# Turned tiles handed on by halves, modulated tiles by inner tile, and the expert routing pulled ahead of the rounds' loop

## The reference

```python
# first block, two layers
for layer in range(2):
    y = mixer_block(x, ...)                         # projections, four branches, gates, output projection
    x = layer_norm(ALPHA * x + y, ln_g[layer, 0], ln_b[layer, 0])
    y = swiglu(x, ffn_w1, ffn_w3, ffn_w2) if layer == 0 else moe_ffn(x, ...)
    x = layer_norm(ALPHA * x + y, ln_g[layer, 1], ln_b[layer, 1])

def moe_ffn(x, router_w, router_b, w1, w3, w2):      # 8 experts, 2 for each token
    logits = x @ router_w + router_b
    top_val, top_idx = top_k(logits, 2)
    weights = softmax(top_val)
    return sum over experts of combine[e] * swiglu(x, w1[e], w3[e], w2[e])

# second block, two layers
for l in range(2):
    sh_a, sc_a, g_a, sh_f, sc_f, g_f = split(silu(c) @ w_mod[l] + b_mod[l], 6)
    h = rms_norm(x, norm_mix[l]) * (1 + sc_a) + sh_a
    x = x + g_a * (attention(h @ w_in[l]) @ w_out[l])
    h = rms_norm(x, norm_ffn[l]) * (1 + sc_f) + sh_f
    x = x + g_f * ((silu(h @ w_gate[l]) * (h @ w_up[l])) @ w_down[l])
```

## Time and profile before

| What | Value |
|---|---|
| Time of three runs, median (lowest to highest) | 2186.43 us (2185.7 to 2187.35) |
| The profiled execution's own time | 2190.64 us |
| Its span | 2188.7 us |
| Mean granted TensorE clock, share of full speed | 0.983 |
| Busy: PE, DVE, ACT, POOL | 96%, 40%, 17%, 4% |
| DMA | 421.44 MB, mean 193 GB/s |

### The profile page before, as it was taken

The page is one execution under the profiler, slowest core; times in us unless marked ns, Lnnn a source line. Parts: engine busy times, 40 slices in busy tenths (PEclk is TensorE's granted clock), DMA queues, the critical chain, the costliest instruction groups (busy, mean ns, idle before and its releaser), DMA issues.

```text
span 2188.7 us, 37442 instructions
## 1 busy us (share of the span) xinstructions
PE 2093.4 (96%) x16270; PEld 1554.7 (71%) x16270; DVE 874.8 (40%) x1695; ACT 374.0 (17%) x891; POOL 78.2 (4%) x180
## 2 busy tenths in 40 slices
PE   9998999999999989999999999899999999999998
PEld 8787786877688867866543554387687768858786
DVE  1415435677724164342010000235466753444443
ACT  1312230000113132301010000133300012431000
POOL 3000000000000000020000000000000020000000
PEclk9999899999999998998999999999999999999999
DMA  8334234588563342337999999852468764233452
GB/s 259 111 99 149 80 123 166 194 302 288 179 194 97 97 164 77 106 99 254 347 319 363 342 336 346 298 170 97 173 234 290 264 197 134 97 116 111 159 173 96
DMA packets 333831, 421.44 MB, mean 193 GB/s; under 512 B 27222, under 2 KB 282148, under 8 KB 333668
## 3 DMA queue, kind: packets, MB, share of 16 engines
q1 hardware_dynamic: 312464, 352.96, 49.7%
q0 software_dynamic: 13408, 50.66, 6.6%
q10 hardware_dynamic: 7796, 15.43, 2.0%
HBM read 417.90 MB, written 1.05 MB: 191 GB/s over the span
## 4 chain that ended last, share of the span: by engine, by line
PE 85%; DVE 5%; DMA 5%; ACT 3%; issue 1%; ACTq 1%; SPq 0%; DVEq 0%; POOL 0%; POOLq 0%
PE psum L1276 14%; PE psum L1308 13%; PE psum L1415 11%; PE psum L1283 9%; PE psum L1293 9%; PE psum L1475 5%; PE psum L1939 3%; DMA ring<-in_w_up 3%; PE psum L1546 3%; PE psum L1721 2%; PE psum L1320 2%; DMA ring<-in_ffn_w 2%; PE psum L1749 1%; PE psum L1404 1%; PE psum L1488 1%
## 5 line engine op out<-in xcount | busy, mean ns | idle before, releaser
L1276 PE MATMUL psum<-xT,ring 128*128 128x256 f32 x1600 | 368.0, 390 | 6.4 <-ACT small L778 4.1
L1276 PEld LDWEIGHTS psum<-xT,ring 128*128 128x128 f32 x1600 | 307.9, 195 | 60.3 <-issue 6.6
L1293 PE MATMUL psum<-ring,arena 128*128 128x512 f32 x528 | 232.1, 593 | 0.0
L1283 PE MATMUL psum<-ring,xT 128*128 128x256 f32 (+2 forms) x960 | 202.5, 369 | 8.7 <-DVE xT L2668 3.9
L1283 PEld LDWEIGHTS psum<-ring,xT 128*128 128x128 f32 x960 | 172.4, 192 | 35.4 <-DVE xT L2668 4.2
L1293 PEld LDWEIGHTS psum<-ring,arena 128*128 128x128 f32 x528 | 97.9, 190 | 111.8 <-issue 111.6
L2115 DVE SCALAR_TENSOR_TENSOR arena<-arena,cond 128x512 f32<-128x512 f32 x168 | 126.3, 752 | 5.5
L1415 PE MATMUL psum<-ring,arena 128*32 128x256 f32 x2304 | 126.8, 379 | 0.7 <-DVE arena L2250 0.7
L1308 PEld LDWEIGHTS psum<-xT,ring 128*128 128x128 f32 x960 | 111.2, 192 | 19.0 <-issue 19.0
L1308 PE MATMUL psum<-oT,arena 128*128 128x128 f32 x960 | 117.6, 276 | 7.0 <-DVE arena L2130 7.0
L1308 PEld LDWEIGHTS psum<-oT,arena 128*128 128x128 f32 x960 | 112.0, 192 | 8.0 <-DVE arena L2130 8.0
(11 more groups left out here) (417 smaller groups left out, 2528.1 us busy)
## 6 DMA issues: line engine op xcount, KB each, us to landing
ring<-in_w_in SPq DMA_DIRECT2D x80, 1024.0 KB, 5.7
ring<-in_exp_w SPq DMA_DIRECT2D x312, 256.0 KB, 6.2
arena<-in_w_mod POOLq DMA_DIRECT2D x48, 1024.0 KB, 9.3
ring<-in_ffn_w SPq DMA_DIRECT2D x33, 1024.0 KB, 7.1
arena<-in_exp_w SPq DMA_DIRECT2D x120, 256.0 KB, 7.0
ring<-in_w_gate SPq DMA_DIRECT2D x22, 1024.0 KB, 8.1
ring<-in_w_up SPq DMA_DIRECT2D x22, 1024.0 KB, 10.6
ring<-in_w_down SPq DMA_DIRECT2D x22, 1024.0 KB, 5.1
```

Of the source, the lines that this page charges most:

```text
L1276: ins = pe.matmul(dst, w[:, k * 256 + c0:k * 256 + c0 + m], act_t[:, k, :], start=(k == 0), stop=(k == KT - 1))
L1283: ins = pe.matmul(dst, act_t[:, k, t * P:t * P + P], w[:, k * 256 + c0:k * 256 + c0 + n], start=(k == 0), stop=(k == KT - 1))
L1293: ins = pe.matmul(psum[:, 4 + 2 * t + h, :], gT[:, s % 2, f * 256 + t * P:f * 256 + t * P + P], w2[:, f * D + h * 512:f * D + h * 512 + 51 ...
```

## The change

- `turn` and `turn_scaled` signal twice, after inner tiles 3 and 7. ACT's copy of the first bank and DVE's part of the modulation start on the first signal.
- PE waits inside the first product of a tile: for the copied tiles ahead of `k` = 0 and `k` = 4 (`copied`), for the modulated ones ahead of every `k`, in the order 0, 4, 1, 5, 2, 6, 3, 7 (`modulated`). `arrived` puts the waits into the first product only.
- `turn_scaled` always writes banks 2 and 3, so that products in banks 0 and 1 may start before a bank has been read out; the modulation columns move from bank 3 to bank 1.
- The router's logits, the two largest and their places are found tile by tile, and each tile's router matmuls have a bank and a job of their own.
- DVE: `rounds` is worked out ahead of the ranked codes; three pairs of small instructions become one each; the softmax weights come last. The gather matrix of the first round is made ahead of the loop (`pick`, two instructions for each tile in place of three), that of a next round at the end of the round before. In the last round it is made in vain.
- `yb` is copied in three instructions, and each scattering matmul waits for its own.
- The layer norm's sums over halves of `acc` are taken inside the loop, as the halves are done (`half_sums`). After it DVE aggregates both tiles, normalises tile 0, only centres tile 1 (`centred`), modulates tile 0 and then finishes tile 1 (`norm_scaled`).

```diff
             def transposed(tag, t):
-                act.wait_ge(*ready("pe_job", "xt", *tag, t))
                 for j in range(2):
+                    act.wait_ge(*ready("pe_job", "xt", *tag, t, j))
                     step(act.copy(xT[:, 4 * j:4 * j + 4, t * P:t * P + P],
...
                 def keep_rows_of(q, d):
                     act.wait_ge(*ready("x_pe", "y", q, d))
-                    xstep(act.copy(yb[:, d], psum[:, 3 * d:3 * d + 3, :]), "y", q, d)
+                    for r in range(3):
+                        xstep(act.copy(yb[:, d, r, :], psum[:, 3 * d + r, :]), "y", q, d, r)
...
             def turn_scaled(which, l, t):
                 for k in range(KT):
-                    ins = pe.matmul(psum[:, 2 * t + k // 4, (k % 4) * P:(k % 4) * P + P],
+                    ins = pe.matmul(psum[:, 2 + k // 4, (k % 4) * P:(k % 4) * P + P],
                                     x[:, t, k * P:k * P + P], diag[:, t, :], start=True, stop=True)
-                job(ins, "xt", which, l, t)
+                    if k % 4 == 3:
+                        job(ins, "xt", which, l, t, k // 4)
+
+            def copied(tag, t):
+                def wait(k):
+                    if k % 4 == 0:
+                        pe.wait_ge(*ready("act", "xt", *tag, t, k // 4))
+                return range(KT), wait
 
             def modulated(which, l, t):
-                pe.wait_ge(*ready("dve", "modulated", which, l, t))
-                pe.wait_ge(*ready("act", "modulated", which, l, t))
+                def wait(k):
+                    pe.wait_ge(*ready("dve" if k < 4 else "act", "modulated", which, l, t, k))
+                return (0, 4, 1, 5, 2, 6, 3, 7), wait
+
+            def arrived(order, wait, n):
+                for k in order:
+                    if n == 0:
+                        wait(k)
+                    yield k
...
                 def scatter_rows(q, d, t):
-                    if t == 0:
-                        pe.wait_ge(*ready("x_act", "y", q, d))
                     for r in range(3):
+                        if t == 0:
+                            pe.wait_ge(*ready("x_act", "y", q, d, r))
...
                 dve.wait_ge(*ready("pe_job", "ranks"))
-                for c in range(2):
-                    step(dve.tensor_tensor(ranked[:, :, c, :], onehot[:, :, c, :],
-                                           psum[:, 5, 0:16].rearrange("p (t e) -> p t e", t=NT), ALU.mult))
                 step(dve.tensor_reduce(most[:, 0:1], psum[:, 5, 16:24], AX, ALU.max))
                 step(dve.tensor_scalar(rounds[:, 0:1], most[:, 0:1], float(ROOM), 1.0, ALU.is_gt, ALU.add))
-                step(dve.tensor_scalar(rounds[:, 1:2], most[:, 0:1], float(2 * ROOM), None, ALU.is_gt))
-                step(dve.tensor_tensor(rounds[:, 0:1], rounds[:, 0:1], rounds[:, 1:2], ALU.add))
+                step(dve.scalar_tensor_tensor(out=rounds[:, 0:1], in0=most[:, 0:1], scalar=float(2 * ROOM),
+                                              in1=rounds[:, 0:1], op0=ALU.is_gt, op1=ALU.add))
                 step(dve.tensor_copy(rounds_i[:], rounds[:]), "rounds")
...
+                def pick(t, done):
+                    done(dve.tensor_scalar(other[:], number[:], code[:, t, 1:2], None, ALU.is_equal))
+                    return dve.scalar_tensor_tensor(out=gather[:, t, :], in0=number[:], scalar=code[:, t, 0:1],
+                                                    in1=other[:], op0=ALU.is_equal, op1=ALU.add)
+                for t in range(NT):
+                    pick(t, step).then_inc(*made("x_pick", "first", t))
...
             for l in range(DEPTH):
                 if l == 0:
+                    for t in range(NT):
+                        norm_sum(t, "ln2", 1)
                     dve.wait_ge(*ready("rows", "ln2", 1))
-                    norm_sums(acc, 0, "ln2", 1)
                     norm_rows(acc, 0, "ln2", 1)
-                    norm_sums(acc, 1, "ln2", 1)
                     scaled("mix", l, 0)
-                    norm_rows(acc, 1, "ln2", 1)
+                    centred(acc, 1, "ln2", 1)
...
                 modulate("mix", l, 0)
+                if l == 0:
+                    norm_scaled(1, "ln2", 1)
```

More of the change, by code:

```diff
@@ L1741, in _ @@
                     turn(x, ("b1", l), t, ("ln", "ln2", 0) if l == 1 else None)
-                    pe.wait_ge(*ready("act", "xt", "b1", l, t))
+                    order, wait = copied(("b1", l), t)
                     for n, i in enumerate(RWKV_IN[0:2]):
@@ L1747, in _ @@
                             o = j * 256 + t * P
-                            for k in range(KT):
+                            for k in arrived(order, wait, n + j):
                                 ins = pe.matmul(psum[:, RAW_BANK[i], o:o + P],
@@ L1970, in _ @@
                     turn_scaled("mix", l, t)
-                    modulated("mix", l, t)
+                    order, wait = modulated("mix", l, t)
                     for n in range(2):
```

129 lines of the change are left out of this document (75 added, 54 removed).

## The result

| | median of the runs | span, profiled execution | time, profiled execution |
|---|---|---|---|
| before | 2186.06 us (4 runs, 2184.83 to 2187.35) | 2188.7 | 2190.64 |
| changed | 2172.49 us (4 runs, 2166.42 to 2173.13) | 2171.4 | 2173.13 |

The ratio is 0.9932 with a 95% interval of 0.9913 to 0.995: 13.6 us faster, where 21.3 were forecast. In a second series the same kernel had 2169.62 us (6 runs) against 2189.69 (14 runs of before), ratio 0.9908 (0.9892 to 0.9925), 20.1 us. The change is faster, the hand-overs gained what they were priced at or a little less, and the measured median lies inside the stated range of 2160 to 2174, near its upper end.

The account below looks back on a forecast made before the run. PE, busy 96% of the span, was taken as the bound, so only its waits could yield gains. The terms for hand-overs, router, experts' end and clock summed to 21.3 us: 2186.4 - 21.3 = 2165.1 us, range 2160 to 2174.

Parts of the forecast that it names:

- Copied tiles: Six hand-overs of turned, copied tiles: PE's wait falls from 1.16 to about 0.18 us, gaining 0.98 us each.
- Layer 0's 1.1: First block, layer 0 projections: only tile 0's gain, 1.1 us, counts; tile 1's is lost waiting for a parameter transfer.
- Router: Router stage: 1.7 us gained, 1.1 from tile 1's hand-over and 0.6 from the ranks to `rounds`.
- possible bonus: Router's stretch: up to 3 us more if it gets its full clock back earlier.
- the 0.6 for the chain to `rounds`: Router, DVE from the ranks to `rounds`: four small instructions instead of seven gain 0.6 us.
- End of the experts: Passage out of the experts: 0.9 us from waiting for a smaller copy, 0.6 from earlier sums, together 1.5.
- Second block, layer 0: Second block's first layer, modulated tiles: tile 0 gains 2.1 us, tile 1 gains 0.5.
- The clock's 1.7: Second block's first product group: full clock instead of half once the second gap goes, 1.7 us gained.
- Gated feed-forwards and layer 1's projections: Second block's modulated tiles: four gated tiles gain 1.37 us each, 5.5; the second layer's two projection tiles gain 3.2.
- The broken stream: Rival, chance 0.16: waits at inner tiles break PE's matmul stream, 10.2 us come back, giving 2175.3 us.
- The transfers: Rival, chance 0.12: feed-forward transfers do not move with PE, so 5.9 us are waited away, giving 2171 us.
- The half clock: Rival, chance 0.03: longer idle between the router's tiles spreads half clock through gather and first expert block, giving 2195 us.

Follow-up runs that it names:

- copied_only: The kernel before with only the copied (not scaled) tiles handed on by halves: 2184.41 us, ratio 0.9977 to before.
- second execution: The changed kernel timed and profiled again with no edit: 2169.62 us, ratio 0.9908 to before.
- start_kept: The changed kernel with 9 small identity matmuls, results unused, ahead of layer 0's wait for the positions: 2167.31 us, ratio 0.9888 to before.
- rest_only: The changed kernel with both hand-overs, copied and modulated tiles, whole again: 2187.86 us, ratio 0.9991 to before.
- less_filled: The changed kernel with fewer filling identity matmuls in the router, 5 instead of 8 and 8 instead of 18: 2166.9 us, ratio 0.9901 to before.
- waits_everywhere: The changed kernel with the same waits ahead of every product of a tile, 164 more: 2174.13 us, ratio 0.9918 to before.
- router_kept: The changed kernel with start_kept's and less_filled's edits, plus identity matmuls in the router's idle gaps (14 instead of 5, and 6): 2164.26 us, ratio 0.9879 to before.

## Why the prediction was right, step by step

*Copied tiles.* Right, 0.83 to 0.93 us each instead of 0.98 (copied_only; the same waits stand in the changed kernel's trace). ACT's copy took 0.60 us on the chain, not 0.54, and PE started 0.04 behind it. The sum priced two of the six, layer 0's and the router's, at 1.1, more than its own working gave.

*Layer 0's 1.1.* The step that failed in the profiled execution. The prediction named the transfer that takes tile 1's gain and gave the longer wait no price beyond that. The transfer ended 0.8 us earlier, PE arrived 1.9 us earlier and stood 1.80 us instead of 0.71, and behind it ran at half clock. Cost there 5.3 us against the forecast. In the second execution 2.0.

*Router.* Forecast 1.7; 2.1 by the trace of the changed kernel, 2.65 by the second, 0.8 by start_kept's. The mean granted clock of the stage, from the router's first product to the gather, sorts them. It is 0.60 in all four traces without the halved hand-over (25.6 to 25.9 us), and 0.70 or 0.71 in six of the seven that have it and all the identity matmuls (23.0 to 23.7 us); the seventh, start_kept, has 0.59 and took 24.83. So at like clock the router's part is worth 0.8 to 1.1 us, less than forecast, and the rest of the 2.1 is a piece of half clock that was gone, which the prediction had only as a possible bonus. It comes with the hand-over: copied_only alone has 25.62 - 23.67 = 1.95. Of the 0.6 for the chain to `rounds`, 0 to 0.3 reach the gather (rest_only), since the identity matmuls behind it then run longer at half clock. The gather matrix ahead of the loop is worth nothing, as said, and less_filled shows that the cover was the identity matmuls.

*End of the experts.* Right: 0.9 and 0.6 as 0.9 and 0.59 in the last column, and 0.90 and 0.59 in the second execution. The Trainium skill, Perfetto Trace Analysis, section Optimizing Scalar/DVE Operations, has each instruction pay its data access anew, and says of an engine that is not saturated but makes another one wait that breaking up its instructions may help. The trace agrees with both: three copies took 1.56 us against 1.44 for one, so the split costs ACT 0.12 us, none of it reaches PE (its twelve records took 5.42 us, before 5.41), and PE waits 0.71 us instead of 1.63. The prediction took only the first half of that section, by which its sum would lose 0.2 us.

*Second block, layer 0.* Tile 0 2.0 for 2.1, and it takes both parts of the change. The clock's 1.7 came, and the three against eleven traces carry its reason. At tile 1 the 1.75 us in front of the products went. Behind them PE waits 0.85 us for bank 0's release, and with the 0.17 us at inner tile 4 the products take 1.2 us longer up to the next work. By the last column 7.5 - 6.9 = 0.6 us stays, for 0.5 forecast.

*Gated feed-forwards and layer 1's projections.* Forecast 1.37 for each of four tiles and 3.2 for two. From one turning to what follows its products the gated tiles took 1.32, 1.34, 1.34 and 1.32 us less, and the projections' two tiles 1.50 and 1.54.

*The rivals.* The broken stream is excluded, by waits_everywhere. The Trainium skill's page TensorE: Matmul & The Clock Gate, section Step-by-step: what each phase is for, has PE pull weight loads ahead of matmuls in flight; with a satisfied wait at each inner tile the rows show no sign that this ends (7.19 us with or without). The transfers, 5.9 us, are 0 to 1.8 in the second block and at most 0.8 in the first. The half clock did not spread beyond the gather.

*The size.* The terms but the clock's 1.7 make 19.6 us; the last row of the table has 15.6, 14.8 in the second execution, 16.2 in start_kept's. In the first execution the last column puts the missing 4.0 us so: 0.3 at the start, 0.9 over the copied tiles (0.4 of it at the hand-overs, 0.3 at transfers), 2.2 in the router, and some 0.6 in the second block. The router's 2.2 are mostly the column's doing: the stage took 2.1 us less, yet in the column it loses 0.5, because PE there waits for DVE and taking off half of all half-clock time takes too much. So it cannot be said to better than about 2 us how much of the forecast stayed away. Beyond that the clock decides: between two executions of one kernel it moves 4 to 9 us, as much as a quarter to a half of the change.

*What stays open.* Two executions of start_kept took 2157.54 and 2159.83 us at mean clocks of 0.987 and 0.986, 8 to 10 us below the profiled one at 0.986; the clock does not explain them. Nor was it tried what lets the clock fall behind the router's tile 1 and in the attention of layer 0, where it was at half level for 17 us of the trace of before (239 to 250 and 260 to 267 us) though no wait of PE is listed there.

## What to carry to other kernels

Where a stage hands a whole tile to the next engine, price the hand-over from the last producer's end to the first consumer's start, and split until the next piece arrives within the consumer's work on the one before. The added waits cost nothing measurable here when they were satisfied. Ask also what lies behind the stage: in the router the shorter chain mostly went into identity matmuls that were only there to fill. Arriving early at a transfer need not be neutral: it lengthens an idle gap, and in both traces where the gap came near 1.8 us the work behind it ran at half clock. When an engine's wait recurs with one length (1.16 us, five or six times), look at what the releasing engine itself waited for: here it was the transfer, so the price of a late transfer was the sum of two rows.

## What the runs showed of the hardware that was not expected

The mean granted clock alone moves one kernel by up to some 9 us between executions (0.981 to 0.985 in before). It fell behind the gaps of 1.78, 1.80 (positions) and 2.19 us (second block) in all five traces that had one, behind the gap of 2.06 us near 57 us in eight of fourteen, and behind none of the 1.75 us ahead of the gated tiles; in router_kept it fell with a gap of only 0.40 us, behind matmuls of 8 columns. In the second block's first gated feed-forward it fell behind the two longest waits for `ring<-in_w_up`, 2.83 us (the changed kernel) and 2.85 us (rest_only), and behind none of the other waits for it there, the longest of them 2.22 us (copied_only). Nor is filling a gap free: 18 identity matmuls, partly at half clock, held the gather back by 5.6 to 6.7 us, and in the changed kernel's trace its matrix was ready 3.2 us before it started.
